# Seven block products in place of two tiles for four more input chunks of a hybrid layer (chunks 15 to 18)

## The reference, cut to what matters

```python
u = rmsnorm(h, norm_mix_w[layer])
proj = (u @ w_in[layer]).astype(jnp.float32)
(hq, hf, hi, hg, mq, mk, mv, mo, mi, mf, sz, sxbc, sdt) = split_last(proj, IN_SPLITS)
y_a = hgrn2_mixer(hq, hf, hi, hg, lower_bounds[layer], hg_norm_w[layer])
y_b = mlstm_mixer(mq, mk, mv, mo, mi, mf, ...)
y_c = mamba2_mixer(sz, sxbc, sdt, ...)
h = h + jnp.concatenate([y_a, y_b, y_c], axis=-1) @ w_out[layer]
h = h + hierarchical_moe(rmsnorm(h, norm_ffn_w[layer]), ...)
```

## Time and profile before

| | before |
|---|---|
| median of three runs | 1471.69 us |
| profiled execution, its time | 1472.66 us |
| its span, first to last instruction | 1470.9 us |
| PE busy | 1263.2 us (86%) |
| VectorE busy | 539.7 us (37%) |
| ACT busy | 217.0 us (15%) |
| GpSimd busy | 215.7 us (15%) |
| mean granted clock of PE | 0.925 |

### The profile page before, as it was taken

The page is one execution under the profiler, slowest core; times in us unless marked ns, Lnnn a source line. Parts: engine busy times, 40 slices in busy tenths (PEclk is TensorE's granted clock), DMA queues, the critical chain, the costliest instruction groups (busy, mean ns, idle before and its releaser), DMA issues.

```text
span 1470.9 us, 20527 instructions
## 1 busy us (share of the span) xinstructions
PE 1263.2 (86%) x8658; PEld 758.4 (52%) x8658; DVE 539.7 (37%) x1204; ACT 217.0 (15%) x372; POOL 215.7 (15%) x159
## 2 busy tenths in 40 slices
PE   9999999999999999867876887688768777877797
PEld 7898899879999994322322232222223222322243
DVE  3554567434633215732322232223222322232225
ACT  3212414112150013000000000000000000001003
POOL 3180055016535721000000000000000000000000
PEclk9999999999999999987998788888889988898899
DMA  8653354445358669999999999999999999999998
GB/s 240 215 172 101 92 145 130 145 138 165 123 176 304 237 225 387 433 431 431 430 434 430 433 432 430 433 430 434 430 433 432 430 433 430 433 430 429 432 428 341
DMA packets 106903, 487.60 MB, mean 331 GB/s; under 512 B 20012, under 2 KB 91976, under 8 KB 92776
## 3 DMA queue, kind: packets, MB, share of 16 engines
q1 hardware_dynamic: 104320, 481.01, 81.0%
q0 software_dynamic: 1392, 5.47, 1.0%
q10 hardware_dynamic: 1130, 0.24, 0.1%
HBM read 482.36 MB, written 4.61 MB: 331 GB/s over the span
## 4 chain that ended last, share of the span: by engine, by line
PE 52%; DMA 45%; DVE 1%; issue 1%; POOL 1%; ACT 0%; SPq 0%; DVEq 0%; POOLq 0%
DMA big<-in_moe_w_dram 43%; PE bank L1769 23%; PE bank L2213 7%; PE bank L2128 5%; PE bank L2246 3%; PE bank L2259 3%; PE bank L1882 2%; PE bank L2182 2%; PE bank L2226 1%; PE bank L1919 1%; PE bank L1895 1%; DMA big<-in_w_in_dram 1%; PE bank L1961 1%; DMA big<-in_x_dram 1%; DVE big L1253 0%
## 5 line engine op out<-in xcount | busy, mean ns | idle before, releaser
L2213 PE MATMUL bank<-big 128*32 128x512 f32 x2016 | 293.0, 735 | 184.7 <-DMA big<-in_moe_w_dram 183.5
L1769 PE MATMUL bank<-big 128*128 128x128 f32 (+4 forms) x2288 | 361.2, 318 | 1.3 <-DVE colc L1190 0.5
L1769 PEld LDWEIGHTS bank<-big 128*128 128x128 f32 x2288 | 322.3, 191 | 31.0 <-issue 1.6
L2213 PEld LDWEIGHTS bank<-big 128*32 128x32 f32 x2016 | 72.7, 131 | 400.5 <-DMA big<-in_moe_w_dram 208.2
L1601 DVE COPY big<-bank 128x512 f32<-128x512 f32 x32 | 22.1, 691 | 497.9 <-PE bank L2213 497.6
L1614 DVE TENSOR_TENSOR big<-big,bank 128x512 f32<-128x512 f32 x240 | 146.1, 679 | 12.4 <-PE bank L2259 12.4
L2259 PE MATMUL bank<-big 32*128 32x512 f32 x480 | 127.0, 633 | 0.7 <-ACT big L1038 0.7
L2246 PE MATMUL bank<-big 128*32 128x512 f32 x992 | 124.6, 647 | 0.6 <-issue 0.3
L732 POOL COPY big<-big 32x512 f32<-32x512 f32 x4 | 2.4, 602 | 763.4 <-ACT big L1071 763.2
L2259 PEld LDWEIGHTS bank<-big 32*128 32x128 f32 x480 | 46.8, 183 | 61.8 <-DVE big L1614 41.3
L2246 PEld LDWEIGHTS bank<-big 128*32 128x32 f32 x992 | 31.5, 117 | 88.1 <-issue 87.6
(11 more groups left out here) (356 smaller groups left out, 1043.5 us busy)
## 6 DMA issues: line engine op xcount, KB each, us to landing
big<-in_moe_w_dram SPq DMA_DIRECT2D x91, 4096.0 KB, 32.8
big<-in_w_in_dram SPq DMA_DIRECT2D x25, 2048.0 KB, 8.2
big<-in_w_out_dram SPq DMA_DIRECT2D x7, 2048.0 KB, 8.2
big<-in_moe_w_dram SPq DMA_DIRECT2D x7, 2048.0 KB, 13.4
big<-in_moe_w_dram SPq DMA_DIRECT2D x6, 1024.0 KB, 9.0
h_rows<-big SPq DMA_DIRECT2D x1, 2176.0 KB, 14.3
big<-gate_rows POOLq DMA_DIRECT2D x8, 272.0 KB, 4.6
big<-h_rows SPq DMA_DIRECT2D x1, 2176.0 KB, 13.1
```

Of the source, the lines that this page charges most:

```text
L1769: last = V.matmul(outs, a, b, start=start and j == 0, stop=stop and j == n - 1)
L2213: last = V.matmul(pb[2 + r][CAP * g:CAP * (g + 1), :], xsT[:, k % 4, k // 4, :], wk, start=j == 0, stop=j == 3)
```

## The change

Four chunks are added to the tuple FOLD. Nothing else is edited: the code around it already asks whether a chunk is in FOLD.

```diff
--- before.py
+++ after.py
@@ -233,7 +233,7 @@
         oh = part(13056, NA * CAP).rearrange("p (a s) -> p a s", a=NA)
         wo = part(13120, NA * P).rearrange("p (a c) -> p a c", a=NA)
         wT = part(13376, NA * P)
-        FOLD = (4, 5, 6, 11, 12, 13, 14, 19, 20, 21, 22, 23, 24)
+        FOLD = (4, 5, 6, 11, 12, 13, 14, 15, 16, 17, 18, 19, 20, 21, 22, 23, 24)
         NF = len(FOLD)
         HT = T // 2
         START, cur = [], 0
```

## The result

The median went from 1471.74 us (four runs, 1471.09 to 1471.80) to **1485.67 us** (four runs, 1485.35 to 1485.71): 13.9 us more, a ratio of 1.0093 with a 95% interval of 1.0082 to 1.0105. The forecast was 1486, range 1477 to 1492. The profiled execution took 1485.66 us, its span 1483.8, mean granted clock 0.913 after 0.925.

What follows compares the result with a forecast made beforehand. PE was taken to bound the stretch around chunks 15 to 18: stalls of 17.8 us less 7.3 from matmuls gave +10.5, plus 4 for the clock +14.5, so about 1486 us, range 1477 to 1492.

Steps and rivals of the forecast that it cites:

- PE sets the pace, a shift there is a shift of the end: Around chunks 15 to 18 PE is always busy, so its shift at 332 us moves the end one for one.
- The matmuls give 7.3 us: Folded products save PE 1.9 us each in chunks 15, 16, 17 and 1.6 in chunk 18, together 7.3 us.
- Decays and scores get through one per GpSimd instruction: In the head pairs, one VectorE decay or score passes at each end of a GpSimd subtraction.
- (b): Rival: exclusion looser, decays or 16x16 instructions slip through, +5.7 or +8.4, with some clock 1477 to 1482 us; chance 0.16.
- (c): Rival: no collision, only chunk 18's sums late, 1470 to 1472 us, no change; chance 0.05.
- slower: Outcome that the whole kernel's time rises, given a chance of 0.90.
- Pair 0, 0.2 us: First head pair: scores 0 held under chunk 15's sums until 272.0, past PE's four products; 0.2 us lost.
- The walk: Step-by-step reckoning of PE's stalls through chunks 15 to 18: 17.8 us lost, less 7.3, chunk 19 starts 10.5 later.
- Pair 1, 6.9 us: Second head pair: four of scores 1 held under sums 16 until 285.6, PE ready at 278.8; 6.9 us lost.
- Chunk 17, 4.8 us: Decays 4 held under sums 17 delay adds_b(16), so chunk 17's second product waits; 4.8 us lost.
- Chunk 18, 5.4 + 0.5 us: Sums 18 stand behind GpSimd's wait for all eight decays; PE loses 5.4 us for the second, 0.5 for the third.
- The clock, +4 us: After each of three stalls PE may return at its lower clock, 1.3 us each, +4 us.

Runs made afterwards that it cites:

- 1: Changed kernel with GpSimd's subtractions for chunks 15, 16 and 17 cut to one column of one block (outputs wrong): 1527.01 us.
- 5: Changed kernel with each GpSimd subtraction for chunks 15, 16 and 17 cut into four pieces: 1474.57 us.
- 11: Changed kernel with chunk 18's sums ahead of the wait for the eighth decays and subtractions for chunks 15 to 18 in two pieces: 1470.10 us, ratio 0.9987.
- 6: Changed kernel with chunk 18's sums, uncut, moved ahead of GpSimd's wait for the eighth decays and of the floor rows: 1484.40 us.
- 2: Against the kernel before, only chunk 18 added to FOLD, not 15, 16 and 17: 1478.70 us.
- 3: Changed kernel with matmuls that compute nothing filling PE's three gaps (chunks 16, 17 and 18): 1480.18 us.
- 4: Changed kernel with VectorE making adds_b of chunks 14 to 17 before, not behind, the decays of pairs 0, 2, 4 and 6: 1480.14 us.
- experiment 10: Changed kernel with chunk 18's sums ahead of the wait for the eighth decays and subtractions in four pieces from chunk 11 on: 1465.04 us, ratio 0.9953.

## Why the prediction was right, point by point

- **PE sets the pace, a shift there is a shift of the end.** Held in all eleven rows of the table, within 0.7 us. (The first rows were misread on the way: expert weights are 43% of the chain, not over half. Nothing in the sum hangs on it.)
- **The matmuls give 7.3 us.** They gave 6.4. A folded chunk of 136 columns takes 13.4 us with its handovers, not 7 x 1.88, and one of 128 columns 12.9, not 12.6.
- **Decays and scores get through one per GpSimd instruction.** Shown: by taking the sums away (1), by cutting them in four and in two (5, 11), and by moving them onto other decays (6). The rule of the Trainium skill ("SBUF — State Buffer", section "Who interferes with whom"), that a VectorE instruction with two SBUF inputs or in a two-port mode and a GpSimd one that reads SBUF exclude each other for the whole instruction, agrees with the traces: among scores 1 even a 16x16 one took 2.32 us. No run shows in which mode the decays ran. Rivals (b) and (c) fall. (The terms that (b) names for its second case give +8.9, not +8.4, and the chances of "slower" add to 0.91; neither matters here.)
- **Pair 0, 0.2 us.** Nothing was lost. Scores 0 ended at 271.2, not 272.0; half of that is the 0.4 us by which this execution was ahead, the rest GpSimd, whose subtractions the walk had set 2.6 us apart and which came every 2.3 to 2.5.
- **Pair 1, 6.9 us.** This step failed in its place and size. I had scores 1 start at 274.5 with two of them through when sums 16 began. They started at 273.74, 1.0 us ahead of sums 16 (274.75) and not 0.5. Four had started by then, a fifth still got in front of GpSimd, and only the last was held. What was held instead were decays 2 (7.61 us), and behind them adds_b(15), so PE lost 4.5 us at the second product of chunk 16. It is the mechanism that the walk gives for chunk 17, one chunk earlier. Half a microsecond more between the two starts, and one score that slipped in, moved the wait from one waiter to another.
- **Chunk 17, 4.8 us:** 3.8, same place, same releaser. Here GpSimd began (297.46) just as scores 3 ended, and the decays took 9.72 us: four of the six went at GpSimd's four ends, the last two right behind. The walk had held three.
- **Chunk 18, 5.4 + 0.5 us:** 5.8, all of it for the second sum. Shown to be the sums' place by 2. The late third sum, predicted to cost 0.5, was covered: at the lower clock the third product lasted longer than a subtraction. In the filled kernel, at full clock, a gap of 0.34 us for it appears.
- **The clock, +4 us:** 5.9, shown by 3 to be the clock. This term was too small: I took the mildest row after an idle of 6 us, 1.3 us a gap, and the gaps cost 1.5 to 2.7 us each, in other kernels up to 3.0. The Trainium skill ("TensorE: Matmul & The Clock Gate", section "Why this matters for your kernels") warns that an idle gap in mid-kernel brings the half clock back. The rows agree for the idles of 3.62 to 6.73 us in these kernels; those of 1.39 to 2.11 us (4, 11) left the granted clock at 1.00.
- **The sum.** 14.1 + 5.9 - 6.4 = 13.6 us for the stretch, forecast 17.8 + 4 - 7.3 = 14.5. The way and the mechanism were right; that the number is so close is luck. Stalls too large by 3.7 us were made up for by a clock too small by 1.9 and a gain of the matmuls too large by 0.9, and in the stalls a wait that never came (pair 1) stood in for one that wasn't foreseen (the second product of chunk 16).

## What to carry to other kernels

Work moved to GpSimd is paid by VectorE where both run: here each float32 VectorE instruction with two SBUF inputs, and each TENSOR_SCALAR within SBUF, waited for the end of the GpSimd subtraction under way, so a chain of six short ones grew from 1.31 us to as much as 9.72. Before placing such work, look who stands behind that chain in VectorE's order, and make GpSimd's instructions short: quartering them for three chunks cut a loss of 14 us to 3. And look where the work stands in GpSimd's own program: one wait for an unrelated event cost PE 6 us of idle and some 2 of clock. Moving the sums without cutting them gave no more than 1.3 us. With both, the loss became a gain of 5.4 us, and of 7.1 with the pieces in the chunks from 11 on as well.

## What the runs showed of the hardware that was not expected

- VectorE passed GpSimd once more at the start. The first subtraction of sums 16 is recorded from 274.75 while scores 1 ran, with 2.81 us instead of 2.35 (3.03 in the kernel with the adds ahead); the fourth score was under way then, and the fifth, at 275.0, still got in before the sixth was held. In these traces "one at each end" describes a GpSimd that is already at work, and not its first instruction.
- Cutting has a price on GpSimd: sixteen pieces took 11.1 us for chunk 19 with VectorE mostly quiet, and 12.4 to 12.8 us among the pairs, where four whole ones take 9.4 (chunk 19) and 9.7 to 9.9. GpSimd in the kernel of experiment 10, in order of time, chunk 18 and chunk 19:

```profile
305.23 12.75 POOL L668 TENSOR_TENSOR big<-big 128x256 f32<-128x256 f32 x16 [2.25 <-PE bank L1778]
...
320.63 11.12 POOL L668 TENSOR_TENSOR big<-big 128x256 f32<-128x256 f32 x16 [2.15 <-DVE big L1345]
```

- The clock's price of a gap isn't fixed by its length: 5.62 us of idle cost 1.5 us of slow clock in the changed kernel, 2.2 in the one with only chunk 18 and 2.7 in the one with pieces (5). Even the gap before chunk 16's second product, with the same program up to it, cost 2.7 us in the changed kernel (285.75) and 1.7 in experiment 6:

```profile
285.74 7.50 PE L1770 MATMUL bank<-big 128*128 128x136 f32 x48 [4.26 <-DVE big L1209]
```

  What decides between them was not tried. So where such gaps are left, 1 us between the single times of two kernels isn't yet a difference of what was edited.
